# Softmax weights scaled before their transposition in both prompt attentions, with the sparse mixer's query blocks reversed and its threshold search shared out anew

## The reference, cut to what matters

```python
def sink_softmax(logits, sinks):          # mixer B
    s = sinks.astype(jnp.float32).reshape(KV_HEADS, GROUP, 1, 1)
    m = jnp.maximum(jnp.max(logits, axis=-1, keepdims=True), s)
    e = jnp.exp(logits - m)
    return e / (jnp.sum(e, axis=-1, keepdims=True) + jnp.exp(s - m))
...
    logits = jnp.where((dist >= 0)[:, :, None, None, :], logits, NEG)   # mixer A
    p = jax.nn.softmax(logits, axis=-1).astype(v_sel.dtype)
    o = jnp.einsum('btngj,btjnd->btngd', p, v_sel)
...
    _, sel = lax.top_k(scores, topk)      # mixer A, samples: 256 of 2056 scores
```

## Time and profile before

| | |
|---|---|
| time before, median of 3 (lowest, highest) | 2341.65 us (2341.57 to 2344.51) |
| the profiled execution: its own time | 2343.02 us |
| the profiled execution: its span | 2341.2 us |
| mean granted clock of PE | 0.982 of 2.4 GHz |
| busy share of the span: PE, DVE, ACT, POOL | 96%, 49%, 18%, 44% |

### The profile page before, as it was taken

How to read it: one execution, slowest core, us unless ns; L and a number is a source line. 1 busy time by engine, 2 the same in 40 slices (tenths; PEclk the granted TensorE clock), 3 DMA queues, 4 the chain that set the end, 5 groups by cost and what they waited for, 6 DMA issues and landing times.

```text
span 2341.2 us, 39794 instructions
## 1 busy us (share of the span) xinstructions
PE 2258.6 (96%) x14801; PEld 2029.8 (87%) x14819; DVE 1137.1 (49%) x1811; ACT 415.4 (18%) x848; POOL 1029.7 (44%) x622
## 2 busy tenths in 40 slices
PE   7999999999888899999999999999999999999997
PEld 6999989959666588999999999999996689999997
DVE  4544522488584546555512555542264465555311
ACT  3101000131554412010000101000015420101002
POOL 4546455414001024555555555555541055555552
PEclk9999999999799999999999999999999899999998
DMA  5435363535003433333223333322350023333221
GB/s 125 99 73 115 78 155 89 114 64 147 10 1 100 130 89 77 86 81 81 78 84 90 82 86 85 81 78 82 94 154 23 1 73 81 81 86 83 79 83 60
DMA packets 378042, 196.33 MB, mean 84 GB/s; under 512 B 66531, under 2 KB 374476, under 8 KB 377932
## 3 DMA queue, kind: packets, MB, share of 16 engines
q1 hardware_dynamic: 366108, 180.79, 31.3%
q10 hardware_dynamic: 11552, 13.71, 2.0%
q0 software_dynamic: 288, 0.56, 0.1%
HBM read 192.23 MB, written 11.64 MB: 87 GB/s over the span
## 4 chain that ended last, share of the span: by engine, by line
PE 61%; DVE 2%; ACTq 0%; ACT 0%; issue 0%; DVEq 0%
PE psum L594 17%; PE psum L597 11%; PE psum L595 10%; PE psum L593 10%; PE psum L596 9%; PE psum L749 1%; PE psum L775 1%; DVE XS L1448 1%; PE psum L745 1%; PE psum L789 1%; ACTq L1200 0%; PE psum L758 0%; DVE squares L1481 0%; PE psum L939 0%; PE psum L938 0%
## 5 line engine op out<-in xcount | busy, mean ns | idle before, releaser
L545 POOL CAST WSP<-WST 128x1024 fp32r<-128x1024 f32 (+1 forms) x305 | 310.5, 1018 | 1250.0 <-PE psum L597 1008.8
L547 POOL TENSOR_TENSOR WSP<-WST,WSP 128x1024 fp32r<-128x1024 f32 (+1 forms) x305 | 709.3, 2326 | 24.5
L594 PE MATMUL psum<-XS,WSP 128*128 128x512 f32 x1672 | 658.4, 394 | 0.0
L593 PE MATMUL psum<-XS,WSP 128*128 128x320 f32 x1672 | 520.4, 311 | 9.5 <-DVE XS L1448 4.3
L597 PE MATMUL psum<-XS,WSP 128*128 128x320 f32 x1672 | 522.7, 313 | 0.0
L595 PE MATMUL psum<-XS,WSP 128*128 128x320 f32 x1672 | 519.2, 311 | 0.0
L596 PE MATMUL psum<-XS,WSP 128*128 128x256 f32 x1672 | 474.0, 283 | 0.0
L596 PEld LDWEIGHTS psum<-XS,WSP 128*128 128x128 f32 x1672 | 314.8, 188 | 71.5
L593 PEld LDWEIGHTS psum<-XS,WSP 128*128 128x128 f32 x1672 | 321.4, 192 | 11.6 <-DVE XS L1448 5.2
L597 PEld LDWEIGHTS psum<-XS,WSP 128*128 128x128 f32 x1672 | 321.5, 192 | 0.0
L594 PEld LDWEIGHTS psum<-XS,WSP 128*128 128x128 f32 x1672 | 314.4, 188 | 0.4
(11 more groups left out here) (325 smaller groups left out, 2595.0 us busy)
## 6 DMA issues: line engine op xcount, KB each, us to landing
WST<-in_ffn_w_gate SPq DMA_DIRECT2D x168, 256.0 KB, 3.9
WST<-in_ffn_w_up SPq DMA_DIRECT2D x168, 256.0 KB, 3.9
WST<-in_ffn_w_down SPq DMA_DIRECT2D x192, 224.0 KB, 3.5
WST<-in_a_w_in SPq DMA_DIRECT2D x28, 256.0 KB, 4.4
kv0A<-in_cache_kv SPq DMA_DIRECT2D x48, 128.0 KB, 2.3
kv2A<-in_cache_kv SPq DMA_DIRECT2D x48, 128.0 KB, 2.3
WST<-in_b_w_in SPq DMA_DIRECT2D x20, 256.0 KB, 4.0
kscr<-in_cache_idx SPq DMA_DIRECT2D x128, 32.0 KB, 2.1
```

What stands on the lines that cost most here:

```text
L545: nc.gpsimd.tensor_copy(WSP[s][:, 0, 0:width], WST[s][:, 0:width]).then_inc(w_hi, 1)
L547: nc.gpsimd.tensor_tensor(WSP[s][:, 1, 0:width], WST[s][:, 0:width], WSP[s][:, 0, 0:width].bitcast(F32), ALU.subtract).then_inc(w_split, 1)
L593: mm(front, high, x[:, 0, 0:FRONT], start=first, stop=False)
L594: mm(split, high, x[:, :, FRONT:TOK], start=first, stop=False)
```

## The change

1. **Weights scaled ahead of the transposition.** The per-block chain (inverse, 16 matmuls, copy, product) goes. For each unit DVE inverts 2 sums per row, and the weights are multiplied by them in place before PE turns them: by POOL in A (2 operations of 128 x keys each), by DVE in B. DVE's order becomes maximum of u, inverse of u-1 (B: and the 2 products), search step. PE's order becomes L(u+2), V(u-1), T(u). High and low parts of the output come straight out of PSUM, the high one always on ACT.
2. **Sink as a column.** In B the bias strips get two more columns, sink minus far bias and a mask value, so that maximum and sum hold the sink.
3. **A's blocks run 3, 2, 1, 0.**
4. **The search.** `FOUND = 9`: count 0 is taken at k = 0, and steps follow from k = 1 to 9. Counts 1 to 9 are ACT's, 10 to 23 (units 0 to 13) DVE's, 24 to 30 (units 14 to 20) ACT's, 31 DVE's; the three closing pieces come at units 22, 23 and 24.
5. **`block_diagonal` of A moves to POOL**, behind the products of unit 1.
6. **Samples.** In A, PE turns the first keys ahead of `new_logits`, waiting for all but the last output half; in B the wait for the outputs moves behind the logits. POOL's splits for the projection out wait for its last product.

```diff
             pool.dma_start(mixers["A"]["selb"].rearrange("s h b r -> s (h b r)"), io["c_selb"])\
                 .then_inc(MS["A"]["selb_in"], 16)
-            pool.wait_ge(MS["A"]["qk_ps"], NQT * GRP)
+            m, ms = mixers["A"], MS["A"]
+            for u, (i, g) in enumerate((i, g) for i in ORDER["A"] for g in range(GRP)):
+                pool.wait_ge(ms["ri_set"], u + 1)
+                for n in range(KVH):
+                    if u or n:
+                        pool.wait_ge(ms["pn_set"], 2 * u + n)
+                    p = m["p"][:, u % 2, n, 0:key_range("A", i)[1]]
+                    nc.gpsimd.tensor_scalar(p, p, m["ri"][:, i, n, g:g + 1], None, ALU.mult).then_inc(ms["pn_set"], 1)
+                if u == 1:
+                    pool.wait_ge(ms["pn_set"], 4)
+                    block_diagonal(m, ms)
+            pool.wait_ge(MS["A"]["pn_set"], 2 * NQT * GRP)
...
-                for u, (r, i, g) in enumerate(units):
-                    more = u + 2 < len(units)
-                    transposed(u)
-                    if g == GRP - 1:
-                        row_scales(r, i)
-                    elif more:
+                for u in range(len(units)):
+                    if u + 2 < len(units):
                         logits(u + 2)
                     if u:
                         values(u - 1)
-                    if g == GRP - 1 and more:
-                        logits(u + 2)
+                    transposed(u)
                 values(len(units) - 1)
...
-                if FOUND + 1 + u <= SIGN_COUNTS:
+                if u in SIGN_UNITS:
                     count(FOUND + 1 + u)
...
+                def factors(u):
+
+                    r, i, g = units[u]
+                    dve.wait_ge(ms["p_set"], 2 * (u + 1))
+                    nc.vector.reciprocal(m["ri"][:, i, :, g], m["rs"][:, i, :, g]).then_inc(ms["ri_set"], 1)
+                    if L == "B":
+                        dve.wait_ge(ms["ri_set"], u + 1)
+                        for n in range(KVH):
+                            p = m["p"][:, u % 2, n, 0:key_range(L, i)[1]]
+                            ts(p, p, m["ri"][:, i, n, g:g + 1], None, ALU.mult).then_inc(ms["pn_set"], 1)
+
+                def low_part(r, h):
+
                     i = ORDER[L][r]
+                    s = (slice(0, P), slice(4 * h, 4 * h + 4), slice(i * P, (i + 1) * P))
+                    dve.wait_ge(ms["oh_set"], 2 * r + h + 1)
+                    tt(XL[s], bank[6 + h].rearrange("p (g t) -> p g t", g=4), XH[s].bitcast(F32), ALU.subtract)\
+                        .then_inc(ms["ot_evac"], 1)
...
-ORDER = {"A": (0, 1, 2, 3), "B": (3, 2, 1, 0)}
-BITS, SIGN_COUNTS, FOUND = 32, 16, 7
+SINK = {"A": 0, "B": 2}
+STRIP = {L: 2 * P + SINK[L] for L in "AB"}
+ORDER = {"A": (3, 2, 1, 0), "B": (3, 2, 1, 0)}
+BITS, FOUND, SIGN_UNITS = 32, 9, range(14, 21)
+SIGNED = (*range(1, FOUND + 1), *(FOUND + 1 + u for u in SIGN_UNITS))
```

More of the change, by code:

```diff
@@ L557, in ffn, with block_diagonal @@
                         split(n0 + GU_CHUNKS + q, i, RING, DB * P)
+            def block_diagonal(m, ms):
+                pool.wait_ge(acc_evac, at["inA"][1] + A_CHUNKS + RING)
+                nc.gpsimd.memset(m["qbd"][:, :, :], 0.0).then_inc(ms["qbd_clear"], 1)
+                pool.wait_ge(ms["qbd_clear"], 1)
+                for n in range(KVH):
+                    h = slice(n * HD, (n + 1) * HD)
+                    dst = m["qbd"][h].rearrange("p b (n g t) -> p n g b t", n=KVH, g=GRP)[:, n]
+                    nc.gpsimd.tensor_copy(dst, m["qT"][h, :, SEQ:TOK].rearrange("p g (b t) -> p g b t", b=NB))\
+                        .then_inc(ms["qbd_set"], 1)
+                pool.wait_ge(ms["qbd_set"], KVH)
             ffn("ffn0")
@@ L751, in logits @@
                     ins.then_inc(ms["qk_ps"], 1)
[L753 to L761, removed]
                 turned = turned_counts(L)
@@ L883, in paged_sample_attention @@
                 keys(0, 2)
+                new_logits()
                 logits(0, 0)
@@ L1237, in prompt_attention @@
                         exps(u + 1)
-                    if L == "A" and r and g == 2:
-                        high_parts(r - 1)
-                    if L == "B" and g == GRP - 2:
-                        act.wait_ge(ms["es_in"], r + 1)
-                        fn(m["es"][:, :, :], m["es"][:, :, :], ACT.Exp).then_inc(ms["es_set"], 1)
                     nk = key_range(L, i)[1]
@@ L1256, in prompt_attention @@
                     after(u)
-                    if g == GRP - 1:
-                        scales(r)
-                if L == "A":
-                    high_parts(NQT - 1)
+                    if g == 5:
+                        high_part(r, 0)
+                    if g == 1 and r:
+                        high_part(r - 1, 1)
+                high_part(NQT - 1, 1)
             def paged_sample_attention(m, ms):
@@ L1593, in prompt_attention @@
                         between(r)
[L1594 to L1596 removed]
+                    nk = key_range(L, i)[1] + SINK[L]
                     dve.wait_ge(ms["qk_ps"], u + 1)
[L1598 to L1610 removed]
+                    nc.vector.tensor_reduce(m["nm"][:, i, :, g], PS[u % 2][:, :, 0:nk], AX, ALU.max, negate=True)\
+                        .then_inc(ms["nm_set"], 1)
+                    if u:
+                        factors(u - 1)
+                    if g == 7:
+                        low_part(r, 0)
                     if g == 3 and r:
[L1612 removed]
+                        low_part(r - 1, 1)
                     after(u)
[L1614 to L1616 removed]
+                factors(len(units) - 1)
+                low_part(NQT - 1, 1)
             def paged_sample_attention(m, ms):
@@ L1906, in selections @@
                     sample_mask()
-                elif k == BITS + 2:
-                    block_diagonal(m, ms, a0 + A_CHUNKS)
             ranks = squares.rearrange("p a t -> p (a t)")[:, 0:SEGW]
```

106 lines of the change are left out of this document (26 added, 80 removed).

## The result

The changed kernel takes 2359.86 us (median of four runs, 2357.84 to 2364.68), the kernel before 2342.57 in runs beside it: ratio 1.0076, 95% interval 1.0062 to 1.0091. It got 17.3 us slower where I forecast 7.6 faster; the time lies above my range. The profiled execution of the changed kernel, at 2364.68, is 4.8 above its median and has a span of 2362.9 against 2341.2, 21.7 more. In the experiments 76 more runs of the kernel before gave 2334.66 to 2350.47, medians 2340.3 to 2343.5 by chip, so differences of a few us between medians are read through the ratios. Time also shifts ahead of the stretches that were changed: the first evacuation of `inA` began at 532.63 before and at 533.96 after, and in the profiles of the 16 experiments anywhere from 528.93 to 537.32.

A forecast was written before the change was run, and what follows sets the result against it. PE, busy 96% of the span, was taken to bound the kernel. Start +7.5, first unit +5.4, first to last turn -6.4, into the samples -4.6, B -11 gave -9.1; clock +1.5 made -7.6: 2334 us, range 2325 to 2347.

The forecast's parts named there:

- the bound on POOL's product: Attention A's weight product on POOL: taken as 0.35 us at 256 columns to 0.6 at 512, upper ends 0.65 and 1.25.
- The loop: A's units 14 to 20, DVE waiting for ACT's counts: 4.9 us a unit at 256 keys, 5.5 at 384, together 35.5.
- the sum: Whole kernel: stretch terms give -9.1 us, with +1.5 for PE's clock -7.6 against the profiled execution's 2343.02.
- the clock: Attention A: +1.5 us in small units; rival, 1.2 GHz through much of block 3, 0.24 together with a later start.
- the start: Attention A's start: 7.5 us later, from 3.5 of DVE's work, 3.7 for a blocked step and 0.3; upper end 10.
- First to last turn: Attention A, transposition 0 to 31: 116.3 us against 122.7 before, -6.4, low end -9, high end +8.
- slower: POOL multiplies at the subtraction's price: Rival, attention A: loops of units 14 to 20 at 5.7 to 6.5 us, DVE held in block 3; +14, 2348; chance 0.10.
- The stand for count 1: Ahead of A: DVE waits at k = 2 for ACT, behind 16 DMA issues, until 561.3, some 8 us.
- the lock: Ahead of A: POOL's strip subtraction blocks DVE's two-input step at k = 5 for 3.7 us, small ones 0.3.
- First unit: Attention A, start to first transposition: 9 us instead of 3.6, +5.4 (3.8 to 7.5).
- Into the samples: A's last turn to the samples' first matmul: 1.0 us for evacuation and values instead of 5.6, -4.6.
- B: Attention B: shorter breaks between blocks and shorter end, slightly longer start; -11 us (-9 to -12.5).

The follow-up runs named there:

- experiment 11: Changed kernel with POOL's product of key head 1 as a two-tensor multiplication, key head 0's left with one scalar per partition: 2358.94 us.
- experiment 2: Changed kernel with the divisions of A's prompt weights on VectorE instead of POOL: 2352.42 us, ratio 1.0031.
- 16: Changed kernel with both of POOL's products as two-tensor multiplications by the spread inverse: 2354.96 us, ratio 1.0064.
- experiment 3: Changed kernel with none of the units' counts on ScalarE, VectorE taking all seven: 2340.87 us, ratio 0.9987.
- experiment 15: Changed kernel with 8 filler matmuls ahead of the turns of units 15 to 24: 2353.28 us, ratio 1.0057.
- experiment 14: Kernel of 8 with filler matmuls, 2 ahead of the turns of units 14 to 19 and 10 for units 20 to 24: 2324.57 us, ratio 0.9927.
- experiment 4: Kernel before the change, with mixer B's edits only: 2337.92 us, ratio 0.9976.
- 8: Changed kernel with counts 1, 2 and the units' counts on VectorE, and each unit's two products split between POOL and VectorE: 2326.76 us, ratio 0.9934.
- 1: Changed kernel with counts 1 and 2 of the search on VectorE: 2351.24 us, ratio 1.004.
- 6: Kernel of experiment 3 with ScalarE's 16 DMA issues spread, two behind each of counts 1 to 8: 2335.36 us, ratio 0.9963.
- 12: Changed kernel with FOUND = 7 alone: 2349.19 us, ratio 1.0036.
- 13: Kernel of 10 with POOL's product as a two-tensor multiplication by the spread inverse: 2331.95 us, ratio 0.9956.
- 10: Kernel of 8 with A's blocks first to last and FOUND = 7: 2321.72 us, ratio 0.9913.

## Why the prediction was wrong, by its own steps

**The step that failed** first of all is the bound on POOL's product: "I take 0.35 (256) to 0.6 (512)", with the subtraction's 0.65 and 1.25 as the upper ends. It took about 0.97 at 256 (two in 1.94) and 1.56 at 512, over both ends. I reasoned from the number of tensor inputs; experiment 11 shows that the form with one input is dearer than that with two (1.04 at 512, inside my bound). What I drew from the Trainium skill ("GPSIMD Engine Reference", "Engine selection": one-input work about at line rate, two-input work about twice as slow as VectorE's) points the wrong way for this form: the product with one tensor input took 1.56 at 512 on POOL and 0.48 on DVE (experiment 2). The measurement decides. The loop takes two products: six pairs of 256 columns at 1.94, where my sum had 0.76, and one of 384 at 2.58, where about 0.95 would stand between my two prices: 6 x 1.18 + 1.63 = 8.7.

This step alone doesn't carry the time out of my range: with 8.7 more the sum gives some 2343, and with the product on VectorE the kernel still took 2352.42 (experiment 2). The next largest terms that failed are the clock (6.4, in A's last block and B's samples) and the start (5.4).

**First to last turn**, by the parts of my sum: block 3 35.1 (33.1 forecast), block 2 20.8 (20.7; my terms for DVE there add up to 3.42, not 3.45), units 14 to 20 44.3 (35.5), units 21 to 24 17.4 (15.6), the rest 14.6 (11.4). Of the 15.9 in all, the loop is 8.8, the price just worked out. The loop as such, which waits close it and in which units, was right (experiments 2 and 16), and so was its worth: I wrote that these counts "cost 14 of what the rest earns"; experiment 3 gave 19, and taking it away undoes the whole loss. My rival "slower: POOL multiplies at the subtraction's price" was this mechanism, at 2348 and a chance of 0.10. Its chance and its size were too low, since the upper bound was taken for a bound and wasn't one, and since it was priced alone, with the clock left out.

**The clock** was a rival for block 3, and +1.5 in the sum. It stayed high in block 3 and fell in the loop units instead. In block 0 it cost 3.2 against my 1.9 a unit, 4.5 against what filled waits give (experiment 15). It falls behind PE's waits ahead of block 0 (experiments 14 and 15). The dear product isn't needed for it: with the last block first and the waits left unfilled, block 0 ran at 1.2 GHz without the product on POOL (2) and without the loop (3) as well. The 3.8 in the samples of B are a separate part, for which I had nothing; it comes and goes from kernel to kernel whatever A holds (experiment 4), and its cause stays open. What I cited of the Trainium skill ("TensorE: Matmul & The Clock Gate", "The HAM clock gate": activity opens the gate) agrees with both runs with filled waits: from 690 to 700 the granted clock was 1.00 in experiment 14, and 0.50 in 8, which has the same waits unfilled.

**The start**: +12.9 instead of +7.5. The stand for count 1 was 8.52 as forecast (experiments 1, 6 and 12 remove it). The count came at 563.15 instead of 561.3, 1.3 of that from ahead of the first evacuation: +1.85. The two-input step was held for 0.27 at k = 2, 1.91 at k = 3, 1.04 at k = 4, 3.07 at k = 5 and 1.02 at k = 6, 7.3 in all, where I had 4.0: +3.3. Those at k = 3 and 4 end with weight subtractions of POOL, those at k = 5 and 6 with its two strip subtractions; I had the one at k = 5, and that at k = 3 in my upper end only. The last 0.3 lie between the last evacuation and PE. So the lock was right, and the number of collisions was the mis-sized term.

**First unit**: 9.8 for 9, +6.2 for +5.4. Near, with a value that I had picked between 7.4 at 2.4 GHz and 11 at 1.2; the clock there was 0.85. **Into the samples**: -3.7 for -4.6, 1.94 instead of 1.0, with PE at 1.2 GHz. **B**: -8.1 for -11. The breaks between its blocks went as forecast (4.89, 4.89 and 4.33 became 2.29, 2.29 and 1.99); the first unit cost 1.6 instead of 0.6, the turns 7.0 less instead of 8.6, among other things because a unit in four still waits 0.13, and the end 2.7 less instead of 3.0. My working there has a slip: 3.9 less 0.7 is 3.2. Alone B measured 5.6.

In sum: of the miss of 29 us between the sum and the profiled execution (+21.7 for -7.6), the loop is 8.8, the clock some 3.2 + 0.9 + 3.8 - 1.5 = 6.4 (its price in A's last units, on the way into the samples and in B's samples, less what I had put down), the start 5.4, B 2.9, block 3 with the rest of A 4.7 (2.0 + 0.1 + 1.8 + 0.8), the samples of A 1.2: 29.4. The profiled execution is 4.8 above the median, so the miss of the median is 26; the 1.3 ahead of the first evacuation lie where nothing was changed, and no run shows what brings the 3.8 in B's samples.

## What to carry to other kernels

Where an operation isn't in the trace, its dearest neighbour there is no upper bound unless the form is the same: on POOL, measure a scalar-per-partition multiplication before putting two of them into a loop of semaphores. A step that closes a loop through four engines pays every price at full length: leave the search's counts with the engine that needs their result, even if it is the busier one. And see what an engine has queued (here 16 DMA issues) before asking it for a result two steps earlier; the version with the counts on VectorE, one product for each engine and seven steps found ahead is 0.9% faster than the kernel before (0.9913, 0.9887 to 0.994).

## What the runs showed of the hardware that was not expected

POOL's `tensor_scalar` with a scalar per partition from SBUF, in place, f32: 602 ns at 128 columns, 1243 at 384, 1563 at 512; `tensor_tensor` with a spread operand 398, 826 and 1039 (experiment 11). The faster form holds DVE up: DVE's product with one tensor input, at 384 columns, took 1.08 us beside it (13) and 0.42 beside the slower form (10), though it started 0.04 to 0.06 ahead of POOL's both times; beside the slower form it is POOL's product that is longer, 1.47 instead of 1.24. So here the lock also meets a DVE operation with one tensor from SBUF, and which of the two is held went with the form on POOL. The form that is cheaper on POOL made the kernel 10 us slower. Filling TensorE's waits with matmuls of no use kept 2.4 GHz through block 0 and took its last six units from 14.6 to 9.8 and 10.1 us (14, 15); that the whole kernel gets faster by it is not clear of the scatter.
